# Upper parts first: token-major and expert products take the upper part of a weight load for all its chunks, then its lower part

## The chip, the core and the metric

One NeuronCore of one Trainium2 chip runs the whole kernel. The metric is the device time of one execution in microseconds (us), given as the median of three runs. TensorE is PE in all rows (PEld is its weight load), VectorE is DVE, ScalarE is ACT, GpSimd is POOL, SyncE (which issues the weight loads) is SP. L1717 is line 1717 of the kernel before.

## What is computed

Two transformer layers on 256 tokens of width 1024, in float32. Each layer has three token mixers (gated delta rule, dilated window attention, stick-breaking attention) between an input and an output projection, then a feed-forward part, which is dense in layer 0 and a mixture of 8 experts, two to a token, in layer 1, and then a gate:

```python
for i in range(DEPTH):
    hn = rms_norm(h, attn_norm_w[i])
    h = h + token_mixers(hn, w_in[i], ..., w_out[i])
    hn = rms_norm(h, ffn_norm_w[i])
    if i % 2 == 0:
        h = h + swiglu(hn, ffn_w1[j], ffn_w3[j], ffn_w2[j])
    else:
        h = h + moe_swiglu(hn, router_w[j], moe_w1[j], moe_w3[j], moe_w2[j])
    gate = jax.nn.sigmoid(rms_norm(h, ple_norm_w[i]) @ ple_gate[i])
    h = h + (p[i] @ ple_proj[i]) * gate
return rms_norm(h, final_norm_w)
```

## The kernel before, in words

**Weights in two parts.** Weights stream in loads of 1 MB (128 partitions x 2048 float32) through a ring of six slots, 421 loads in all, of which 336 belong to the experts. For each load ACT writes the upper part `whi` (the value rounded to fp32r, `split_upper`, L622, semaphore `s_hi`, "weights_upper_part_ready"), then DVE writes the rest `wlo = raw - whi` (`split_lower`, L626, semaphore `s_lo`, "weights_split"). The activations are split in the same way into `xh` and `xl`. A product of two such numbers is three matmuls, written out in `product` (L1717 to L1719): upper with upper, upper with lower, lower with upper, all added in one PSUM bank. With token-major operands the activation is the stationary one (loaded by PEld), and the weights move through, 512 (or 396, 384, 256) columns at a time. Rows name these three matmuls `whi,xh`, `wlo,xh` and `whi,xl`.

**The wait.** Before a load's first product PE waits once, in `ready` (L631), for `s_lo`, that is for the lower part, which comes after the upper part.

**Who takes which load.** `both_blocks` multiplies one 512-column group of weights with both blocks of 128 tokens; its eight chunks of the contraction come in two loads ("halves"), four chunks in each. It serves the token-major part of the input projection (J, three groups in a layer), the second half of the output projection (WO) and the gate (PG, two groups): 12 calls, 24 loads. In the experts an item is 128 gathered tokens of one expert. `up` (kinds A and B, seven 512-wide column groups j each) multiplies the gathered tokens with a half of four chunks, twice per group; `down` (kind C, seven groups) multiplies the gated product, turned to chunk-major by four transposes in `turn` (L2090), with a half that feeds both output banks YY0 and YY1. That is 42 loads and 504 matmuls in an item. There are 8 items: seven pass through a loop (`rest_of_item("each")`), the last stands behind it (`rest_of_item("last")`). The loop is turned so that A and B of group 0 of the next item run near the end of this one; A of group 0 stands right behind the last `turn`, ahead of the last `down`. The remaining users of loads (`channels`, the dense layer, the first half of WO, `ple`'s PP) are untouched by the change.

**Order around it.** ACT and DVE run one queue each, in which the splits stand between the drains of PSUM at places fixed by the plan (`Split.behind`). SP issues load n+6 when PE has finished with load n (a signal at the end of a half, or a filled PSUM tile).

Of the kernel before, what the change touches and what calls it, by code (L numbers as in the profile page):

```python
# [15 lines left out]
P = 128  # L16
# [379 lines left out]
def build(nc, x, stream, experts, columns, rows, final_w, consts, out):  # L396
# [9 lines left out]
    with ExitStack() as ctx:  # L406
# [222 lines left out]
        def ready(eng, key, it=None):  # L629

            eng.wait_ge(s_lo, through(load_at[key] + 1, it, per_load))  # L631

# [1054 lines left out]
        def _(pe):  # L1687
# [32 lines left out]

            def x_part(start, width):
                return xh[:, start:start + width], xl[:, start:start + width]

            def both_blocks(keys, name, width, items=None, turned=None):


                for half in range(2):
                    ready(pe, name + (half,), items)
                    for b, key in enumerate(keys):
                        if half == 0:  # L1730
                            opened(key, items)
                        for q in range(4):
                            k = 4 * half + q
                            if b == 0:
                                chunk_ready(turned, k, items)
                            ins = product(bank(key, 0, width), x_part(T * k + P * b, P),
                                          weights(name + (half,), width * q, width), k == 0, k == KC - 1)
                        if half:
                            ins.then_inc(s_fill, 1)
                    if half == 0:  # L1740
                        ins.then_inc(s_used, 1)
# [335 lines left out]
            def up(kind, ph, j, it):  # L2077
                key = (kind, ph, j)
                opened(key, it)
                for half in range(2):  # L2080
                    ready(pe, key + (half,), it)
                    for q in range(4):
                        k = 4 * half + q
                        ins = product(bank(key), x_part(P * k, P), weights(key + (half,), 512 * q, 512), k == 0, k == KC - 1)
# [8 lines left out]
            def down(ph, j, it):  # L2093
# [4 lines left out]
                for half in range(2):  # L2098
                    ready(pe, ("C", ph, j, half), it)
                    for m in range(2):  # L2100
                        for q in range(2):
                            c = 2 * half + q
                            ins = product(bank(("YY", ph, m)), (mTh[j % 2][:, P * c:P * c + P], mTl[j % 2][:, P * c:P * c + P]),
                                          weights(("C", ph, j, half), D * q + 512 * m, 512), j == 0 and c == 0,
                                          j == NJ - 1 and c == 3)
# [140 lines left out]
```

## Time and profile before

| | us |
|---|---|
| median of three runs | 1720.54 (1720.02 to 1720.63) |
| profiled execution, device time | 1722.51 |
| profiled execution, span of the trace | 1720.8 |
| PE busy, share of the span | 1635.3, 95% |
| PE weight load busy | 1392.9, 81% |
| DVE busy | 1296.5, 75% |
| ACT busy | 1047.9, 61% |
| POOL busy | 144.8, 8% |
| mean granted TensorE clock | 0.974 of full |

The profile is of one execution. Its span runs from the first to the last instruction; the device time is 1.7 us more than that. A matmul's busy time in a row is longer than its pace, since matmuls overlap: the pace is read from the start times of neighbouring rows. The stages by time: mixers of layer 0 to about 223 us, dense layer to about 421, gate and mixers of layer 1 to about 657, router and the first gather to about 681, experts to about 1669, gate and final norm to the end.

### The profile page before, as it was taken

The page shows a single profiled execution, that of the slowest core. Times are in us where ns is not written, and L with a number is a line of the kernel's source. Part 1 is how long each engine was busy: PE and PEld are TensorE (multiplying, and loading weights), DVE is VectorE, ACT ScalarE, POOL GpSimd, SP SyncE. Part 2 cuts the span into 40 slices and gives each one's busy share as a digit, 9 for nine tenths or more (in the row PEclk, how much of TensorE's full clock was granted, in tenths as well). Part 3 has the DMA queues.
Part 4 walks back from the last instruction along what each step waited for, and adds up shares of the span by engine and source line. Part 5 has one row for each costly group of instructions (what it writes and reads, how often), then busy time and mean ns, then how long its engine had stood idle before and what let it go on. Part 6 is the DMA issues. An engine that isn't in the chain of part 4 may idle for free.

```text
span 1720.8 us, 23469 instructions
## 1 busy us (share of the span) xinstructions
PE 1635.3 (95%) x8812; PEld 1392.9 (81%) x8812; DVE 1296.5 (75%) x1214; ACT 1047.9 (61%) x1005; POOL 144.8 (8%) x131
## 2 busy tenths in 40 slices
PE   6999989999899986999999999999999999999986
PEld 6989789998798975788887887887878878877864
DVE  4976555556687666788888888888888888888964
ACT  5646243334574724667676767677777767676743
POOL 0134100000012511000000000001000000002000
PEclk9999899999999998999999999999999999999998
DMA  7440154545444012999999999999999999999970
GB/s 287 169 149 1 50 202 178 199 169 220 151 168 171 2 49 86 370 365 357 389 363 360 382 367 359 380 358 382 367 358 383 367 348 392 367 351 411 368 275 25
DMA packets 65713, 459.91 MB, mean 267 GB/s; under 512 B 7408, under 2 KB 7792, under 8 KB 11632
## 3 DMA queue, kind: packets, MB, share of 16 engines
q1 hardware_dynamic: 61904, 445.88, 67.9%
q0 software_dynamic: 3744, 13.13, 2.0%
q8 instruction: 45, 0.74, 0.2%
q14 instruction: 20, 0.16, 0.0%
HBM read 450.58 MB, written 8.40 MB: 267 GB/s over the span
## 4 chain that ended last, share of the span: by engine, by line
PE 89%; DVE 4%; ACT 4%; POOL 1%; DMA 1%; issue 1%; DVEq 0%; POOLq 0%; ACTq 0%; SPq 0%
PE ps L1717 26%; PE ps L1719 26%; PE ps L1718 26%; PE ps L1835 2%; DVE wlo L626 2%; PE ps L1844 2%; ACT whi L622 1%; PE ps L2090 1%; PE ps L1904 1%; ACT xh L1036 1%; PE ps L1833 1%; DMA raw<-in_experts 1%; PE ps L1705 1%; POOL work L747 1%; PE ps L1816 0%
## 5 line engine op out<-in xcount | busy, mean ns | idle before, releaser
L626 DVE TENSOR_TENSOR wlo<-raw,whi 128x2048 fp32r<-128x2048 f32 x421 | 944.8, 2289 | 114.9 <-ACT whi L622 114.6
L622 ACT CAST whi<-raw 128x2048 fp32r<-128x2048 f32 x421 | 782.7, 1916 | 59.3 <-DMA raw<-in_experts 58.9
L1717 PE MATMUL ps<-whi,xh 128*128 128x512 f32 (+3 forms) x1568 | 623.1, 397 | 31.9 <-DVE wlo L626 20.0
L1718 PE MATMUL ps<-wlo,xh 128*128 128x512 f32 (+3 forms) x1568 | 616.3, 393 | 0.0
L1719 PE MATMUL ps<-whi,xl 128*128 128x512 f32 (+3 forms) x1568 | 616.0, 393 | 0.0
L1717 PEld LDWEIGHTS ps<-whi,xh 128*128 128x128 f32 x1568 | 297.6, 190 | 101.2 <-DVE wlo L626 17.3
L1719 PEld LDWEIGHTS ps<-whi,xl 128*128 128x128 f32 x1568 | 297.4, 190 | 67.1
L1718 PEld LDWEIGHTS ps<-wlo,xh 128*128 128x128 f32 x1568 | 298.0, 190 | 64.3
L1717 PE MATMUL ps<-xh,whi 128*128 128x256 f32 x656 | 186.2, 284 | 0.0
L1719 PE MATMUL ps<-xh,wlo 128*128 128x256 f32 x656 | 184.7, 282 | 0.0
L1718 PE MATMUL ps<-xl,whi 128*128 128x256 f32 x656 | 184.7, 282 | 0.0
L1047 ACT ACTIVATE work<-ps 128x512 f32<-128x512 f32 x56 | 33.5, 599 | 200.8 <-PE ps L1719 200.8
L1717 PEld LDWEIGHTS ps<-xh,whi 128*128 128x128 f32 x656 | 123.8, 189 | 1.3 <-issue 0.5
L1718 PEld LDWEIGHTS ps<-xl,whi 128*128 128x128 f32 x656 | 123.7, 189 | 1.4 <-issue 0.5
L1719 PEld LDWEIGHTS ps<-xh,wlo 128*128 128x128 f32 x656 | 123.6, 188 | 0.0
L1125 DVE TENSOR_TENSOR xl<-ps,xh 128x512 fp32r<-128x512 f32 x64 | 44.0, 690 | 73.5 <-ACT xh L1051 63.9
L1013 ACT ACTIVATE work<-ps 128x256 f32<-128x256 f32 x22 | 8.4, 384 | 111.5 <-PE ps L1719 111.5
L747 POOL TENSOR_TENSOR work<-work,cst 128x384 f32<-128x384 f32 x56 | 65.9, 1205 | 95.8 <-PE ps L1825 73.1
L788 POOL DMA_DIRECT2D y_rows<-work x7 | 4.0, 569 | 786.7 <-ACT work L1080 786.7
L1454 DVE TENSOR_TENSOR work<-work,ps 128x256 f32<-128x256 f32 x22 | 9.3, 421 | 67.2 <-ACT work L1013 67.2
L1835 PE MATMUL ps<-work 128*128 128x128 f32 x288 | 44.5, 300 | 1.3 <-POOL work L747 1.0
L957 ACT COPY work<-ps 128x384 f32<-128x384 f32 x48 | 23.1, 482 | 36.5 <-PE ps L1835 33.7
(275 smaller groups left out, 1304.8 us busy)
## 6 DMA issues: line engine op xcount, KB each, us to landing
raw<-in_experts SPq DMA_DIRECT2D x336, 1024.0 KB, 4.8
raw<-in_stream SPq DMA_DIRECT2D x85, 1024.0 KB, 4.9
y_rows<-work POOLq DMA_DIRECT2D x7, 512.0 KB, 5.2
y_rows<-work POOLq DMA_DIRECT2D x1, 2560.0 KB, 9.1
cst<-in_consts SPq DMA_DIRECT2D x1, 1383.5 KB, 13.6
h<-in_x SPq DMA_DIRECT2D x1, 1024.0 KB, 5.0
x_rows<-hn POOLq DMA_DIRECT2D x1, 1024.0 KB, 4.4
out<-work SPq DMA_DIRECT2D x2, 512.0 KB, 2.7
```

The source lines that it names most:

```text
L622: nc.scalar.copy(whi[:, n % RING, :], raw[:, n % RING, :]).then_inc(s_hi, 1)
L626: nc.vector.tensor_tensor(wlo[:, n % RING, :], raw[:, n % RING, :], whi[:, n % RING, :].bitcast(F32), ALU.subtract).then_inc(s_lo, 1)
L747: nc.gpsimd.tensor_tensor(cm[:, GW * g:GW * g + GW].rearrange("p (s i) -> p s i", s=3), mt[:, GW * g:GW * g + GW].rearrange("p (s i) -> p ...
L957: nc.scalar.copy(pbuf[:, at], bank(("P", L, lev, g), 0, GW)).then_inc(s_free["a"], 1)
L1036: ins = nc.scalar.activation(xh[:, P * k:P * k + P], bank(("GA", when, half), P * q, P), ACT.Copy, scale=col(COL_NORM(4) + k))
L1047: nc.scalar.activation(ms[j % 2], bank(key), ACT.Silu).then_inc(s_free["a"], 1)
L1125: nc.vector.tensor_tensor(lo, bank(key), hi.bitcast(F32), ALU.subtract).then_inc(s_free["v"], 1)
L1717: pe.matmul(out, ah, bh, start=start, stop=False)
L1718: pe.matmul(out, ah, bl, start=False, stop=False)
L1719: return pe.matmul(out, al, bh, start=False, stop=stop)
L1835: ins = pe.matmul(bank(key, P * s, P), lhs[:, at], rhs[:, at], start=True, stop=True)
L1844: ins = pe.matmul(packed(bank(key, P // 2 * s, P // 2), lev), lhs[:, at], joined(rhs[:, at], lev, odd), start=True, stop=True)
```

## The change

`product` is split in two for the token-major and the expert products. `upper_products` does the two matmuls of a chunk that read `whi`; `lower_product` does the one that reads `wlo`. For each half, PE waits for `s_hi` (new `upper_ready`), runs the upper products of all its chunks, waits for `s_lo`, and then runs the lower products. In `both_blocks` the lower wait stands behind the upper products of the first token block alone; in `up` behind four chunks (8 matmuls); in `down` behind both output banks (8 matmuls). The number of matmuls and weight loads is as before; only the order of the sums changes.

```diff
+        def upper_ready(eng, key, it=None):
+
+            eng.wait_ge(s_hi, through(load_at[key] + 1, it, per_load))
...
+            def upper_products(out, x, w, start):
+
+                (xu, xd), (wu, _) = x, w
+                pe.matmul(out, xu, wu, start=start, stop=False)
+                return pe.matmul(out, xd, wu, start=False, stop=False)
+
+            def lower_product(out, x, w, stop):
+                return pe.matmul(out, x[0], w[1], start=False, stop=stop)
...
                 for half in range(2):
-                    ready(pe, name + (half,), items)
+                    upper_ready(pe, name + (half,), items)
                     for b, key in enumerate(keys):
                         if half == 0:
                             opened(key, items)
@@
                             k = 4 * half + q
                             if b == 0:
                                 chunk_ready(turned, k, items)
-                            ins = product(bank(key, 0, width), x_part(T * k + P * b, P),
-                                          weights(name + (half,), width * q, width), k == 0, k == KC - 1)
+                            upper_products(bank(key, 0, width), x_part(T * k + P * b, P),
+                                           weights(name + (half,), width * q, width), k == 0)
+                        if b == 0:
+                            ready(pe, name + (half,), items)
+                        for q in range(4):
+                            k = 4 * half + q
+                            ins = lower_product(bank(key, 0, width), x_part(T * k + P * b, P),
+                                                weights(name + (half,), width * q, width), k == KC - 1)
                         if half:
                             ins.then_inc(s_fill, 1)
...
                 for half in range(2):
+                    upper_ready(pe, key + (half,), it)
+                    for q in range(4):
+                        k = 4 * half + q
+                        upper_products(bank(key), x_part(P * k, P), weights(key + (half,), 512 * q, 512), k == 0)
                     ready(pe, key + (half,), it)
                     for q in range(4):
                         k = 4 * half + q
-                        ins = product(bank(key), x_part(P * k, P), weights(key + (half,), 512 * q, 512), k == 0, k == KC - 1)
+                        ins = lower_product(bank(key), x_part(P * k, P), weights(key + (half,), 512 * q, 512), k == KC - 1)
                     ins.then_inc(s_fill if half else s_used, 1)
...
                 for half in range(2):
+                    upper_ready(pe, ("C", ph, j, half), it)
+
+                    def turned_part(q):
+                        c = 2 * half + q
+                        return mTh[j % 2][:, P * c:P * c + P], mTl[j % 2][:, P * c:P * c + P]
+
+                    for m in range(2):
+                        for q in range(2):
+                            upper_products(bank(("YY", ph, m)), turned_part(q), weights(("C", ph, j, half), D * q + 512 * m, 512),
+                                           j == 0 and half == 0 and q == 0)
                     ready(pe, ("C", ph, j, half), it)
                     for m in range(2):
                         for q in range(2):
-                            c = 2 * half + q
-                            ins = product(bank(("YY", ph, m)), (mTh[j % 2][:, P * c:P * c + P], mTl[j % 2][:, P * c:P * c + P]),
-                                          weights(("C", ph, j, half), D * q + 512 * m, 512), j == 0 and c == 0,
-                                          j == NJ - 1 and c == 3)
+                            ins = lower_product(bank(("YY", ph, m)), turned_part(q),
+                                                weights(("C", ph, j, half), D * q + 512 * m, 512),
+                                                j == NJ - 1 and half == 1 and q == 1)
```

The order of PE's instructions at the places that the prediction speaks of follows; `weights_upper_part_ready` is `s_hi`, `weights_split` is `s_lo`, REGISTER_ALU works out a wait's value inside the loop of items. PE, the second half of an expert group in the loop, before:

```order
L631 REGISTER_ALU
L1717 MATMUL ps<-whi,xh 128x512 [waits weights_split]
L1718 MATMUL ps<-wlo,xh 128x512
L1719 MATMUL ps<-whi,xl 128x512
L1717 MATMUL ps<-whi,xh 128x512
L1718 MATMUL ps<-wlo,xh 128x512
L1719 MATMUL ps<-whi,xl 128x512
```

The same place in the changed kernel:

```order
L635 REGISTER_ALU
L1728 MATMUL ps<-whi,xh 128x512 [waits weights_upper_part_ready]
L1729 MATMUL ps<-whi,xl 128x512
L1728 MATMUL ps<-whi,xh 128x512
L1729 MATMUL ps<-whi,xl 128x512
L1728 MATMUL ps<-whi,xh 128x512
L1729 MATMUL ps<-whi,xl 128x512
L1728 MATMUL ps<-whi,xh 128x512
L1729 MATMUL ps<-whi,xl 128x512
L1732 MATMUL ps<-wlo,xh 128x512 [waits weights_split]
L1732 MATMUL ps<-wlo,xh 128x512 x3
```

The wait for the lower part has moved behind eight matmuls, and no further REGISTER_ALU stands ahead of it. PE, the last `down` of the last item, its second half with the scatter matmul (L2140 before, L2172 after) behind it, in the changed kernel:

```order
L635 REGISTER_ALU
L1728 MATMUL ps<-whi,xh 128x512 [waits weights_upper_part_ready]
L1729 MATMUL ps<-whi,xl 128x512
...
L1732 MATMUL ps<-wlo,xh 128x512 [waits weights_split]
L1732 MATMUL ps<-wlo,xh 128x512 x3
L594 REGISTER_ALU
L594 REGISTER_ALU [waits psum_drained_by_scalar]
L2172 MATMUL ps<-work 128x512 [waits psum_drained_by_scalar]
```

The four L1732 are two for YY0 and two for YY1, where before six matmuls of YY0 were followed by six of YY1; the scatter matmul behind them waits for ACT to have drained YY0, as before. PE, the first half of the gate's first group at the end of the kernel, changed:

```order
L635 REGISTER_ALU
L1699 REGISTER_ALU [waits weights_upper_part_ready]
L1699 REGISTER_ALU [waits psum_drained_by_scalar]
L1728 MATMUL ps<-whi,xh 128x512 [waits psum_drained_by_vector]
L1729 MATMUL ps<-whi,xl 128x512
...
L1732 MATMUL ps<-wlo,xh 128x512 [waits weights_split]
L1732 MATMUL ps<-wlo,xh 128x512 x3
L1699 REGISTER_ALU
L1728 MATMUL ps<-whi,xh 128x512 [waits psum_drained_by_vector,psum_drained_by_scalar]
```

Here the first wait of the chain is for the upper part where it was for the lower one; the lower one stands ahead of the last four matmuls of token block 0.

## Rows read from the trace of the kernel before

**Rows 1.** Waits of PE: us in total, times, longest us

```profile
PE ps L1717 <- DVE wlo L626: 20.0, 12, 6.2
```

**Rows 2.** The same, 677 to 1660 us (the experts without their end)

```profile
PE ps L1717 <- DVE wlo L626: 4.0, 9, 0.7
```

**Rows 3.** Windows: stretch, us, busy (x) of PE, PEld, DVE, ACT, POOL, clock, DMA share, GB/s

```profile
922.10:1044.30 122.20, 121.77 (x541) 98.24 (x541) 104.58 (x65) 87.70 (x67) 2.84 (x3) 1.00 0.96 369
```

**Rows 4.** Timeline of PE, two halves of an item: start us, us, instruction

```profile
902.74 0.39 PE L1719 MATMUL ps<-whi,xl 128*128 128x512 f32 x1
902.97 0.40 PE L1717 MATMUL ps<-whi,xh 128*128 128x512 f32 x1
...
908.34 0.39 PE L1719 MATMUL ps<-whi,xl 128*128 128x512 f32 x1
```

**Rows 5.** Timeline at an item's end, with [idle before <-releaser]

```profile
797.56 4.49 DVE L626 TENSOR_TENSOR wlo<-raw,whi 128x2048 fp32r<-128x2048 f32 x2 [0.67 <-ACT whi L622]
...
798.85 0.60 PE L2090 MATMUL ps<-cst,work 128*128 128x128 f32 x4
...
799.91 0.50 PE L1717 MATMUL ps<-whi,xh 128*128 128x512 f32 x1 [0.46 <-DVE wlo L626]
```

**Rows 6.** Timeline of PE, transposes with a product behind that waits for nothing

```profile
909.00 1.04 PE L2067 MATMUL ps<-cst,hn 128*128 128x128 f32 x8
909.79 0.48 PE L1717 MATMUL ps<-whi,xh 128*128 128x512 f32 x1
```

**Rows 7.** Timeline, last item, a half with a late load

```profile
1568.58 2.29 DVE L626 TENSOR_TENSOR wlo<-raw,whi 128x2048 fp32r<-128x2048 f32 x1 [2.58 <-ACT whi L622]
...
1569.80 0.40 PE L1719 MATMUL ps<-whi,xl 128*128 128x512 f32 x1
...
1570.92 0.50 PE L1717 MATMUL ps<-whi,xh 128*128 128x512 f32 x1 [0.72 <-DVE wlo L626]
```

**Rows 8.** Timeline, first weights of the kernel

```profile
16.78 6.70 DVE L626 TENSOR_TENSOR wlo<-raw,whi 128x2048 fp32r<-128x2048 f32 x3 [0.91 <-ACT whi L622]
...
19.12 0.70 PE L1717 MATMUL ps<-whi,xh 128*128 128x396 f32 x1 [5.04 <-DVE wlo L626]
```

**Rows 9.** Windows, start of the kernel

```profile
18.01:24.84 6.83, 5.71 (x17) 5.72 (x18) 6.83 (x4) 4.21 (x3) 0.00 (x0) 0.50 0.92 385
```

**Rows 10.** Timeline, the last item's last down

```profile
1658.21 4.49 DVE L626 TENSOR_TENSOR wlo<-raw,whi 128x2048 fp32r<-128x2048 f32 x2 [1.11 <-ACT whi L622]
...
1660.56 0.80 PE L1717 MATMUL ps<-whi,xh 128*128 128x512 f32 x1 [4.80 <-DVE wlo L626]
...
1661.15 0.63 PE L1718 MATMUL ps<-wlo,xh 128*128 128x512 f32 x1
...
1661.57 0.63 PE L1719 MATMUL ps<-whi,xl 128*128 128x512 f32 x1
```

**Rows 11.** Timeline, end of that down: drain of YY0, scatter matmul

```profile
1667.79 0.59 ACT L1080 COPY work<-ps 128x512 f32<-128x512 f32 x1 [4.21 <-PE ps L1719]
...
1668.97 1.88 PE L2140 MATMUL ps<-work 128*128 128x512 f32 x4
```

**Rows 12.** Timeline, first weights of the last gate

```profile
1683.36 6.70 DVE L626 TENSOR_TENSOR wlo<-raw,whi 128x2048 fp32r<-128x2048 f32 x3 [0.75 <-ACT whi L622]
...
1685.98 0.76 PE L1717 MATMUL ps<-whi,xh 128*128 128x512 f32 x1 [6.20 <-DVE wlo L626]
```

**Rows 13.** Timeline of PE, dense layer, where each L1717 opens another bank

```profile
267.30 0.40 PE L1719 MATMUL ps<-whi,gl 128*128 128x512 f32 x1
267.53 0.40 PE L1717 MATMUL ps<-whi,gh 128*128 128x512 f32 x1
```

**Rows 14.** Windows around idle times of PE

```profile
192.10:198.92 6.82, 5.96 (x16) 4.77 (x17) 2.75 (x5) 0.00 (x0) 4.24 (x3) 0.50 0.00 0
622.58:629.40 6.82, 4.50 (x30) 3.84 (x30) 5.59 (x10) 1.07 (x2) 4.15 (x4) 1.00 0.00 0
...
1659.82:1663.23 3.41, 2.67 (x6) 2.17 (x7) 3.41 (x3) 3.41 (x3) 0.00 (x0) 0.50 0.00 0
```

## Prediction

> **What bounds the kernel.** I read the waits of PE first, since PE is busy for 95% of the span. All the idle time that the change can touch is the time in which PE waited for the lower part of a load: 20.0 us in 12 waits [rows 1]. Next I asked where those 12 are. Nine lie inside the experts and make only 4.0 us [rows 2]; the other three are 5.0, 4.8 and 6.2 us long, one at the kernel's start, one at the last item's last `down`, one at the last gate; their rows stand with their terms. So the experts, which take more than half of the time, are bound by PE's own work: in an item of 122.20 us PE is busy for 121.77 at full clock, while DVE has 104.58, ACT 87.70, and the DMA engines are close to busy at 0.96 [rows 3]. The pace of that work is in start times: 24 products in a row take 5.60 us, 0.233 us each [rows 4]. Nothing in the change removes a matmul, so the gain is in waits and in what the waits do to the clock.
>
> **What the change does to a wait.** ACT has the upper part ready when DVE starts on the lower one, and DVE needs 2.3 us for it. So PE may start up to 2.3 us earlier, if nothing else holds it, and then has eight matmuls (1.9 us at full clock) to run before it needs the lower part. Where DVE had long finished, nothing is gained.
>
> **Term 1, the items, 4.9 us.** Behind the last four transposes of an item stands group A 0 of the next. Its lower part is made from 797.56 on, two loads in 4.49 us, so the first is ready at about 799.85, and PE starts at 799.91 [rows 5]. Its upper part was there at 797.5. The row shows 0.46 us of idle time, but the stall is longer: where nothing is waited for, a product starts 0.79 us after the first of eight transposes [rows 6], so after the first of four it is about 0.36, and 798.85 + 0.36 = 799.21. The stall is 0.70 us. The difference, 0.24, is the time in which a product normally overlaps the matmul ahead. There are seven such places (the other two of the nine are term 2): 7 x 0.70 = 4.9 us. It stays gained if the item has no other wait 0.7 us behind this one. The next half's lower part is there at 802.05 [rows 5], and PE, which comes to that half 12 x 0.233 = 2.8 us after its start, at 802.0, then needs it only 1.9 us later: the cover grows in every half. DVE and ACT have 17 and 34 us to spare in an item.
>
> **Term 2, a late load in the last item, 1.4 us.** The load's lower part starts at 1568.58 and PE, whose last product started at 1569.80, goes on at 1570.92 instead of 1570.03 [rows 7]: 0.89 us. The ninth wait is 4.0 - 7 x 0.43 - 0.72 = about 0.25 in the waits' account, with the 0.24 of term 1 about 0.5. Both upper parts are early enough. Together 1.4.
>
> **Term 3, the kernel's start, 2.3 us.** The upper part is ready at 16.78; PE would start there and not at 19.12 [rows 8]. Against this stand two things. The lower wait is reached after eight matmuls and the lower part comes at about 19.07, so PE stalls again for about 0.5 us. And the clock: from 18.01 to 24.84 the granted clock is 0.50, that is 1.2 GHz, 17 matmuls in 5.71 us or 0.336 each [rows 9]; at full clock I estimate 0.186. With the same low stretch after the change: 8 matmuls by 18.54, then 17.5 in 19.07 to 24.84, 25.5 against 17, 8.5 x 0.186 = 1.6 us. If the clock is back halfway, since PE is now busy through the whole stretch: 3.1 us. If it never falls: 4.1. I take 2.3, between the first two.
>
> **Term 4, the last down, 2.3 us.** Upper part at 1658.21, PE started at 1660.56 [rows 10]: 2.3 us earlier again, at two paces: 0.42 us a matmul at 1.2 GHz [rows 10] against 0.233. Same low stretch (1659.82 to 1666.65): 6.4 matmuls before it, 16 in it, and its 24 end at about 1667.0 instead of 1668.97 [rows 11]: 1.9 us. Clock back at 1663.2: 3.5. No fall: 4.7, of which I count 4.2, since in the code DVE has two more loads to split ahead of the residual sums. From each goes 0.4 us: YY0 used to be full six matmuls ahead of the end, so that ACT's drain of 0.59 us was hidden [rows 11]; now it is two matmuls ahead, and the scatter matmul waits. So 1.5, 3.1 or 3.8; I take 2.3.
>
> **Term 5, the last gate, 2.2 us.** Upper part at 1683.36, PE started at 1685.98, 0.3 us after the lower part was ready, through a chain of waits that stays [rows 12]. New start 1683.7. Same low stretch (1683.72 to 1690.54): 5.3 more matmuls in it and the first one earlier, 1.6 us. Clock back halfway: 2.8. No fall: 4.4. I take 2.2.
>
> **What costs nothing.** The 360 loads concerned (336 + 24) get one more wait on PE each, and the order of the changed kernel shows no extra register instruction ahead of it. A wait that is met costs nothing now: between the last product of a half and the first of the next, which carries a wait, lie 0.23 us like anywhere [rows 4]. New is that two matmuls in a row read the same weights. No row has that; the nearest are the two paces of 512 columns, 0.233 [rows 4] and 0.23 in the dense layer [rows 13], which differ by about 1 ns. On 4032 + 576 = 4608 matmuls 1 ns is 4.6 us, up or down. I take 0 and keep part of it for the range.
>
> **A rule that speaks against it.** In `down` the bank changes three times in a half instead of once. In the dense layer every third matmul opens another bank, and the step to it is 0.23 us, at full clock [rows 13]. The Trainium skill (TensorE: Matmul & The Clock Gate, "A second HAM failure mode: psum-queue depth-cycling") says that cycling through PSUM banks made PE pause between groups so often that its clock went down and up. By that rule some of the halves of `down` would run at 0.42 us a matmul instead of 0.233. This trace doesn't agree: the rule's term is 0 here.
>
> **Sum.** 4.9 + 1.4 + 2.3 + 2.3 + 2.2 = 13.1 us. The profiled execution took 1722.51 us, so it would take 1709.4; the median of the runs shown, 1720.54, lies 1.97 lower, so the forecast is 1707.4. With all low stretches as they are: 1.6 + 1.5 + 1.6 + 6.3 = 11.0 us, 1709.5.
>
> **Rivals.**
> *The clock never falls at the three places.* PE's idle time there goes from 5.0, 4.8 and 6.2 us to 2.7, 2.5 and 3.9. What 2.3 us does is undecided: of two idle times of 2.32 us behind the same code, one is followed by 1.2 GHz (192.10 to 198.92) and the other isn't (622.58 to 629.40) [rows 14]. Against it: at 1659.82 the clock stayed low although PE was busy for 2.67 of 3.41 us [rows 14]. Gain 4.1 + 3.8 + 4.4 + 6.3 = 18.6, 1701.9 us. Chance 0.2, for two of three or all.
> *The items keep their period.* DMA at 0.96 and the order of ACT and DVE could pace the item, so that the 0.70 us comes back as a wait for an upper part. For it: the DMA share [rows 3]. Against it: PE's work alone explains the item, and the wait at its end is all there is. Gain 13.1 - 4.9 = 8.2, 1712.3 us. Chance 0.1.
> *The second wait breaks PE's pipeline: slower.* If the weight load that carries the lower wait could no longer overlap the matmul ahead, each of 360 loads would cost the 0.10 us by which a matmul behind a real wait is longer (0.50 against 0.40) [rows 4, 5]: 36 us, less 13, 1743 us. It decides from 0.05 us a load on. Against it: the met wait at 902.97 [rows 4]. A slower pace of the new order, from 4 ns a matmul on, would end on the same side. Chance 0.07.
> *Gain and a small loss of pace cancel*, 2.5 ns a matmul: within 0.2%, 1720 us, chance 0.05.
>
> **Numbers.** A measurement of this kernel can tell about 0.2%, 3.4 us. The forecast has 0.58, the rivals 0.2, 0.1, 0.07, 0.05. Elsewhere the low stretches may fall otherwise once all work comes 2 us earlier; one more or less of 6.8 us is 3.0 us. The range goes from the first rival, 1701.5, to the smallest gain, 1709.5, with one more low stretch and some loss of pace, 1714.0. Faster 0.88, same 0.05, slower 0.07.
>
> **What would show it.** Right: an item of 121.5 us and no wait of PE for a lower part in it; the first J product at 16.8, with a wait for L626 of about 0.5 us behind eight matmuls; the last gate's first product 2.3 us behind ACT's split start and not 4.6; ACT's drain of YY0 visible ahead of the scatter matmul. Wrong: an item of 122.2 with waits for `whi`, or a step between start times other than 0.233, which moves everything.

## The result, and the profile after

| | before | changed |
|---|---|---|
| median of the runs made together on one chip | 1720.59 us (4 runs) | 1711.2 us (4 runs, 1708.2 to 1713.3) |
| the same, second comparison on another chip | 1719.0 us (17 runs) | 1710.41 us (6 runs, 1707.1 to 1713.2) |
| profiled execution, device time | 1722.51 | 1710.77 |
| its span | 1720.8 | 1709.0 |

PE's line of the profile's page, which answers to 1635.3 and 95% before:

```profile
PE 1632.8 (96%) x8812; PEld 1391.7 (81%) x8812; DVE 1296.2 (76%) x1214; ACT 1048.8 (61%) x1005; POOL 152.7 (9%) x131
```

The ratio is 0.9944 (95% interval 0.9930 to 0.9957), and 0.9948 (0.9935 to 0.9961) the second time: faster by 9.4 and by 8.6 us, where 13.1 were forecast. The time lies in the range, 3.8 us above the forecast.

Waits of PE in the changed kernel (us in total, times, longest us), which answer to [rows 1]; L1728 is the upper product, L1732 the lower one:

```profile
PE ps L1728 <- ACT whi L622: 9.1, 3, 3.9
...
PE ps L2172 <- ACT work L1084: 0.2, 1, 0.2
PE ps L1732 <- DVE wlo L626: 0.2, 1, 0.2
```

20.0 us in 12 waits for a lower part have become 9.1 us in three waits for an upper part, and 0.2 for a lower one. The three are the three long ones of before; the nine of [rows 2] are gone but for that 0.2. Here they are in the timeline (start us, us, instruction, idle before and its releaser), first the kernel's start, which answers to [rows 8]:

```profile
16.68 6.70 DVE L626 TENSOR_TENSOR wlo<-raw,whi 128x2048 fp32r<-128x2048 f32 x3 [0.91 <-ACT whi L622]
...
16.70 0.45 PE L1728 MATMUL ps<-whi,xh 128*128 128x396 f32 x1 [2.72 <-ACT whi L622]
...
18.07 0.53 PE L1729 MATMUL ps<-whi,xl 128*128 128x396 f32 x1
...
18.40 0.53 PE L1728 MATMUL ps<-whi,xh 128*128 128x396 f32 x1
...
19.06 1.65 PE L1732 MATMUL ps<-wlo,xh 128*128 128x396 f32 x4
```

PE starts 0.02 us after the upper part is complete (the moment at which DVE starts on the lower part), and reaches the first lower product at 19.06 without a wait. Windows (stretch, us, busy (x) of PE, PEld, DVE, ACT, POOL, granted clock, DMA share, GB/s) of this place, of the last `down`, of the last gate and of one item; they answer to [rows 9], [rows 14] and [rows 3]:

```profile
17.30:20.70 3.40, 3.40 (x12) 3.10 (x11) 3.40 (x2) 3.40 (x3) 0.00 (x0) 0.50 1.02 429
20.70:24.10 3.40, 3.40 (x21) 3.40 (x20) 3.40 (x3) 1.44 (x1) 0.00 (x0) 1.00 1.01 422
908.48:1029.99 121.51, 121.51 (x543) 98.22 (x542) 104.66 (x64) 87.85 (x67) 4.99 (x3) 1.00 0.97 371
1652.20:1655.60 3.40, 3.05 (x7) 2.49 (x8) 3.07 (x2) 3.40 (x3) 0.00 (x0) 0.51 0.82 328
1676.10:1679.50 3.40, 3.40 (x10) 2.60 (x9) 3.40 (x3) 3.40 (x3) 0.00 (x0) 0.51 0.02 5
```

In this execution the clock falls to 1.2 GHz for 3.4 us and not for 6.8 at all three places: the middle case of each of terms 3 to 5. Other executions differ, as the part on the prediction shows. The item takes 121.51 us, and PE is busy in all of it. The end of an item, which answers to [rows 5]:

```profile
797.72 4.50 DVE L626 TENSOR_TENSOR wlo<-raw,whi 128x2048 fp32r<-128x2048 f32 x2 [0.66 <-ACT whi L622]
...
799.04 0.60 PE L2113 MATMUL ps<-cst,work 128*128 128x128 f32 x4
...
799.40 0.48 PE L1728 MATMUL ps<-whi,xh 128*128 128x512 f32 x1
```

The product starts 0.36 us after the first of the four transposes, with no idle time, and now ahead of the lower part, which is complete at about 799.97. The late load of the last item [rows 7], the last `down` and its scatter matmul [rows 10, 11], and the last gate [rows 12]:

```profile
1573.89 1.19 PE L1732 MATMUL ps<-wlo,xh 128*128 128x512 f32 x4 [0.20 <-DVE wlo L626]
```

```profile
1652.53 8.90 DVE L626 TENSOR_TENSOR wlo<-raw,whi 128x2048 fp32r<-128x2048 f32 x4 [1.10 <-ACT whi L622]
...
1652.55 0.80 PE L1728 MATMUL ps<-whi,xh 128*128 128x512 f32 x1 [2.47 <-ACT whi L622]
...
1659.37 1.07 ACT L1084 COPY work<-ps 128x512 f32<-128x512 f32 x2 [1.45 <-PE ps L1732]
...
1660.01 2.41 PE L2172 MATMUL ps<-work 128*128 128x512 f32 x5 [0.21 <-ACT work L1084]
```

```profile
1672.55 3.75 ACT L622 CAST whi<-raw 128x2048 fp32r<-128x2048 f32 x2
1674.52 2.29 DVE L626 TENSOR_TENSOR wlo<-raw,whi 128x2048 fp32r<-128x2048 f32 x1 [0.75 <-ACT whi L622]
...
1674.82 0.47 PE L1728 MATMUL ps<-whi,xh 128*128 128x512 f32 x1 [3.87 <-ACT whi L622]
```

What remains of the long waits is the part that ends with ACT. In the last rows ACT starts on the load at 1672.55 only. That it isn't the load that is late but ACT's other work of this place was tried (gate_ahead, below).

### The profile page after: what moved, and what is told of

Same layout as the page of the kernel before. It is cut to its first block, busy times and chain, and to the rows that moved or that the text cites. A ratio compares the mean times of both kernels' runs of the same rounds, so it can differ in the third digit from the quotient of the medians.

```text
span 1709.0 us, 23469 instructions
## 1 busy us (share of the span) xinstructions
PE 1632.8 (96%) x8812; PEld 1391.7 (81%) x8812; DVE 1296.2 (76%) x1214; ACT 1048.8 (61%) x1005; POOL 152.7 (9%) x131
## 4 chain that ended last, share of the span: by engine, by line
PE 93%; ACT 2%; DVE 2%; DMA 1%; issue 1%; POOL 1%; DVEq 0%; POOLq 0%; ACTq 0%; SPq 0%
PE ps L1728 21%; PE ps L1732 20%; PE ps L1729 20%; PE ps L1721 6%; PE ps L1723 6%; PE ps L1722 6%; PE ps L1854 2%; PE ps L1863 2%; PE ps L2113 1%; PE ps L1923 1%; PE ps L1852 1%; DMA raw<-in_experts 1%; ACT whi L622 1%; ACT xh L859 1%; PE ps L1709 1%
## 5 line engine op out<-in xcount | busy, mean ns | idle before, releaser
L1728 PE MATMUL ps<-whi,xh 128*128 128x512 f32 (+2 forms) x1536 | 610.2, 398 | 14.3 <-ACT whi L622 9.1
L1729 PE MATMUL ps<-whi,xl 128*128 128x512 f32 (+2 forms) x1536 | 597.1, 389 | 0.0
L1732 PE MATMUL ps<-wlo,xh 128*128 128x512 f32 (+2 forms) x1536 | 415.2, 392 | 0.2 <-DVE wlo L626 0.2
L1728 PEld LDWEIGHTS ps<-whi,xh 128*128 128x128 f32 x1536 | 290.4, 189 | 83.2 <-issue 7.5
L1732 PEld LDWEIGHTS ps<-wlo,xh 128*128 128x128 f32 x1536 | 287.1, 189 | 66.6 <-DVE wlo L626 1.1
L1729 PEld LDWEIGHTS ps<-whi,xl 128*128 128x128 f32 x1536 | 290.6, 189 | 59.0
```

The source lines that it names most:

```text
L1728: pe.matmul(out, xu, wu, start=start, stop=False)
L1729: return pe.matmul(out, xd, wu, start=False, stop=False)
L1732: return pe.matmul(out, x[0], w[1], start=False, stop=stop)
```

## The experiments

Twelve further runs were made: of nine new kernels, and once more of the changed kernel and of two of the nine. Each was timed against the kernel before on the same chip, so that differences are to be read against the "before" of the same line. One execution of each run has a trace. The table has the pieces of time between marks that all traces have: the start of the last token-major matmul of layer 0's input projection ("J"), the transposes of the tokens of the second item ("G") and of the eighth, which are the bounds of six items, the last `turn`, the scatter matmul behind the last `down`, the transposes of the last gate's norm, and the end. "Low" is the time at 1.2 GHz between 24 and 690 us, good to 0.3 us, without what is left of the start's own low stretch. Each other number is a difference of two start times, in us.

| kernel | 0 to J | J to G | low | six items | to last turn | to scatter | norm to end |
|---|---|---|---|---|---|---|---|
| before | 105.14 | 681.7 | 61.2 | 733.18 | 135.16 | 13.81 | 42.89 |
| order_only | 104.34 | 681.2 | 61.2 | 731.38 | 134.63 | 13.42 | 42.15 |
| order_again | 103.78 | 680.4 | 61.2 | 732.82 | 134.93 | 12.76 | 43.42 |
| x_start | 103.47 | 681.9 | 61.2 | 731.70 | 135.12 | 12.65 | 42.32 |
| x_down | 104.81 | 681.6 | 57.8 | 731.75 | 135.36 | 9.60 | 42.08 |
| x_up | 104.25 | 681.2 | 61.2 | 728.40 | 134.14 | 13.08 | 42.38 |
| x_rest | 104.21 | 681.0 | 64.7 | 729.00 | 132.88 | 10.68 | 40.91 |
| changed | 101.84 | 685.1 | 68.0 | 729.04 | 133.47 | 10.53 | 39.98 |
| after_again | 102.14 | 683.6 | 68.1 | 729.00 | 132.88 | 9.60 | 40.04 |
| gate_ahead | 102.70 | 685.3 | 68.0 | 729.04 | 132.88 | 10.69 | 35.17 |
| both_ahead | 103.01 | 682.3 | 61.2 | 729.04 | 133.42 | 8.12 | 35.17 |
| warm | 102.71 | 680.6 | 44.2 | 729.00 | 132.88 | 9.60 | 40.05 |
| best | 101.73 | 681.2 | 51.0 | 729.04 | 132.88 | 8.13 | 35.16 |
| best_again | 101.74 | 680.5 | 51.0 | 729.00 | 132.88 | 8.12 | 35.17 |

### The change, one part at a time

Each of these four kernels has the changed form for some callers, and for the others the loops of the kernel before, with `ready` ahead of everything and `product`. The condition is written into `both_blocks`, the expert product and `down`; here it is for x_start:

```diff
             def both_blocks(keys, name, width, items=None, turned=None):
+                if not (name == ("J", 0, 0)):
+                    for half in range(2):
+                        ready(pe, name + (half,), items)
...
+                                ins = product(bank(key, 0, width), x_part(T * k + P * b, P),
+                                              weights(name + (half,), width * q, width), k == 0, k == KC - 1)
...
+                    return
```

**x_start**: only the kernel's first input projection group is changed.

> The change in the first J product of layer 0 alone; everything else waits as before. Theory (each wait gives back what it cost, and low-clock stretches between 113 and 695 us then fall as chance has it): the first product starts at 16.7 instead of 19.1, 1.6 to 3.2 us gained by the first POOL wait at 110 to 112, one low-clock stretch more or less after that, time 1717 to 1721, and PE waits for L626 in the experts as before (item 122.20). Rival (the new order itself costs pace): 1720.5, no gain at 112 either.

Measured: 1717.07 us against 1720.71 of before, ratio 0.9976 (0.9967 to 0.9984), 3.6 us faster, at the lower end of the expected 1717 to 1721. PE starts at 16.93, and J comes 1.7 us earlier than in the trace of the kernel before, but only 1.0 us earlier than on the mean of the six traces with the late start (104.4). Where the rest of the 3.6 us comes from, the one trace doesn't show.

**x_up**: only the expert products (kinds A and B).

> The change in the expert products A and B alone. Theory: the seven waits at the items' starts and the two in the last item go, item 121.51 instead of 122.20, gain 4.8 + 1.4 = 6.2 us, about 1714.4; first 695 us of the trace as before; the last down and the last gate still start behind the lower part. Rival (pace): the item is longer than 121.51, since its 336 matmuls of A and B run in the new order.

Measured: 1714.25 us, ratio 0.9967 (0.9952 to 0.9982), 6.5 us faster. An item of it, in the columns of the windows above:

```profile
785.47:907.00 121.53, 121.53 (x543) 98.24 (x542) 104.47 (x64) 87.71 (x67) 4.92 (x3) 1.00 0.96 372
```

The six items take 728.4 us; the item is short with `up` alone, as the theory of the seven stalls says, since the group behind an item's last `turn` is one of `up`. The time is the one expected (1714.4), but of the two waits in the last item only one went: at 1573.33 us PE still waits 1.10 us for the lower part of a `down` half.

**x_down**: only `down`.

> The change in the expert products C alone. Theory: item 122.20 as before, only the last down gains, 1.5 to 3.3 us, 1717.3 to 1719; ACT's drain of YY0 shows ahead of the scatter matmul. Rival (bank changes cost): the item is longer than 122.20 by some ns for each of 14 x 2 further bank changes, 0.3 us or more.

Measured: 1717.19 us, ratio 0.9979 (0.9969 to 0.9988), 3.5 us faster, 0.1 us more than the expectation allowed. From the last turn to the scatter matmul it takes 9.60 us; the three kernels that leave this `down` as it was take 12.65 to 13.81. The items take 731.75, in the middle of the four kernels of which PE waits at each item's end (731.38 to 733.18), so `down` gives an item nothing. The 122.20 of the expectation is then too exact a number: an item that nothing has changed, in x_start, has 121.84 to 122.11.

**x_rest**: all but the kernel's first group.

> The whole change without the first J product of layer 0. Theory: the first 680 us as in the kernel before (same waits, same low-clock stretches), then 6.2 + 3.3 + 2.8 = 12.3 us less, about 1708.3, with a smaller spread between runs than the whole change has; then the start's 3.2 us were lost again by the clock in between. Rival (the middle is slower through the new order in J, WO and PG): 1711 or more, and the middle loses time with the start unchanged.

Measured: 1713.54 us, ratio 0.9959 (0.9945 to 0.9973), 7.2 us faster and not 12. The items, the last `down` and the gate have what they have in the changed kernel, 922.5 us from G to the end against 922.05 there. But the expectation was that without the earlier start the clock's pattern would stay that of before, and that the runs would agree better. They don't: five runs lie between 1709.4 and 1715.4. The time is the rival's (1711 or more), while its sign, a slower middle, does not show in the trace: J to G takes 681.0 us. But the traced execution is the fastest of the five, 11.3 us below the kernel before, and the longer ones left no trace. So some 5 us of what the parts promise are missing here too, without the earlier start.

### The order without the earlier start

```diff
         def upper_ready(eng, key, it=None):
 
-            eng.wait_ge(s_hi, through(load_at[key] + 1, it, per_load))
+            eng.wait_ge(s_lo, through(load_at[key] + 1, it, per_load))
```

PE then waits for the lower part ahead of the upper products, so that the order of the products is all that is left of the change. **order_only**:

> The changed kernel's order of products, but PE waits for the lower part ahead of the upper products, as the kernel before did. Theory: the whole gain is the earlier start, and the order (two matmuls in a row on the same weights, four banks changed in a down half instead of two) costs and brings nothing: pace 0.233 us in the items, item period 122.2, the three long waits 5.0, 4.8 and 6.2 us again, time that of the kernel before within 2 us plus up to 1 us for the scatter matmul, which now waits for ScalarE's drain. Rival: the order itself has a price or a gain per matmul, 4608 of them: 0.5 ns is 2.3 us, an item period off by 0.25 us.

Measured: 1724.41 us (12 runs, 1717.85 to 1726.37) against 1719.0, ratio 1.0026 (1.0017 to 1.0035): slower by 5.4 us, which the theory didn't have. But the profiled one was the fastest of the twelve, and shows nothing slow: the three long waits are back, and the items take 731.38. So it was run again, as **order_again**:

> The order without the earlier start once more, since its one profiled execution (1717.85 us) was the fastest of its 12 and the others (1720.1 to 1726.4) had a mean granted clock down to 0.970. Theory: the slower executions lose in low stretches between 24 and 690 us and at the three long waits, not in the experts: item period again 121.9 to 122.2, low time above the 61.2 us of the profiled one by 3 to 14 us, the first 690 us longer by 1 to 5 us than there. Rival: the order makes the experts slower in those executions: item period above 122.4.

Measured: 1720.3 us (12 runs, 1716.3 to 1726.8) against 1719.45, ratio 1.0009 (0.9994 to 1.0023): no difference that can be measured. The profiled execution (1718.87 us) is again not one of the longer ones, which it was meant to catch. What the two traces tell is the pace. The waits of PE in order_only:

```profile
PE ps L1728 <- DVE wlo L626: 19.8, 11, 6.2
```

Two items next to each other in order_only, then one of order_again, then one of the kernel before:

```profile
907.38:1029.20 121.82, 121.38 (x542) 98.59 (x541) 104.44 (x64) 87.73 (x67) 3.16 (x3) 1.00 0.96 370
1029.20:1151.38 122.18, 121.73 (x542) 98.28 (x541) 104.53 (x64) 87.61 (x67) 3.33 (x3) 1.00 0.96 369
```

```profile
906.00:1028.18 122.18, 121.72 (x542) 98.27 (x541) 104.58 (x64) 87.81 (x67) 3.32 (x3) 1.00 0.95 369
```

```profile
786.82:909.00 122.18, 121.72 (x542) 98.27 (x541) 104.56 (x64) 87.73 (x67) 3.19 (x3) 1.00 0.96 369
```

An item of the kernel before and one with the new order alone take the same 122.18 us, with 121.72 of work on PE in both. So the order, the two matmuls in a row on the same weights and the additional changes of the bank cost nothing in the experts, and bring nothing: the 0.5 to 0.7 us of an item are the earlier start. This holds for the experts. Open is why 8 of the 12 executions of order_only and 4 of the 12 of order_again are at 1723.5 to 1726.8 us. Their mean granted clock is 0.970 to 0.975 and that of the others, at 1716.3 to 1721.2, is 0.976 to 0.982, so the time goes with the clock; but none of these 12 left a trace. That the new order brings such executions about more often, outside the experts, is a rival that no run here excludes.

### Where the 3 to 4 us went

**after_again**: the changed kernel again.

> The changed kernel once more, on the chip of the other two. Theory: its low stretches between 24 and 690 us do not come to the same sum each time, so that its runs spread over some 5 us (1708 to 1713 so far), 8 to 11 us below the kernel before. Rival: they are fixed by the program, and the profile shows 68 us of low time with the same 11 stretches again and the segments agree to 0.3 us.

Measured: 1710.41 us, ratio 0.9948 (0.9935 to 0.9961). Here the rival was mostly right: low time comes to 68.1 us again, and 0 to J, J to G and the items agree with the first trace to 0.3, 1.5 and 0.04 us. The seven traces of kernels that lack part of the change take 680.4 to 681.9 us from J to G; the four traces whose code up to G is the changed kernel's take 685.1, 683.6, 685.3 and 682.3, on the mean 2.8 us more. The one with 682.3 (both_ahead) is also the one whose low time is 61.2 and not 68. In their one trace each, neither the earlier start alone (x_start, 681.9) nor the rest alone (x_rest, 681.0) does this.

The traces also show where most of it goes. In the output projection of each layer, four transposes are followed by 2.32 us of idle time and twelve matmuls, up to the next transposes. In layer 1 the changed kernel takes 8.19 us for this:

```profile
619.44 0.61 PE L1968 MATMUL ps<-cst,hn 128*128 128x128 f32 x4
622.37 0.77 PE L1721 MATMUL ps<-whi,xh 128*128 128x512 f32 x1 [2.33 <-issue]
...
627.63 1.34 PE L1968 MATMUL ps<-cst,hn 128*128 128x128 f32 x8
```

and the kernel before 6.12, with the matmuls at full clock [rows 14]:

```profile
624.04 0.61 PE L1949 MATMUL ps<-cst,hn 128*128 128x128 f32 x4
626.97 0.48 PE L1717 MATMUL ps<-whi,xh 128*128 128x512 f32 x1 [2.32 <-issue]
...
630.16 1.06 PE L1949 MATMUL ps<-cst,hn 128*128 128x128 f32 x8 [0.15 <-DVE hn L1378]
```

The same stretch in all 14 traces, in us:

| traces | layer 0 | layer 1 | J to G |
|---|---|---|---|
| before, x_start, x_down, both_ahead | 8.2 | 6.1 | 681.6 to 682.3 |
| order_only, order_again, x_up, x_rest, best, best_again | 6.1 | 8.2 | 680.4 to 681.2 |
| changed, after_again, gate_ahead | 8.2 | 8.2 | 683.6 to 685.3 |
| warm | 8.2 | 7.1 | 680.6 |

The ten traces of the first two lines have 1.2 GHz at one of the two places, the three with 68 us of low time at both. That is 2.1 us of the 3.4 by which these three exceed the seven. both_ahead has the same code up to there and the low clock at one place only, so the program does not fix it.

**warm**: products that nobody reads, issued where PE waits for a norm, to see what the low stretches behind these waits cost.

```diff
                     if c == 0:
+                        for _ in range({1: 4, 3: 5, 4: 4}.get(occ, 0)):
+                            pe.matmul(bank(("T", occ, 0)), ident, cst[:, 0:512], start=True, stop=True)
                         pe.wait_ge(s_hn["a"], occ + 1)
```

> The changed kernel with 4, 5 and 4 extra products of 128 x 512 on TensorE into an unused bank, issued where PE waits for the norms ahead of the second, fourth and fifth sets of norm transposes (the profile shows a granted clock of 0.50 for 3.4 to 6.8 us behind each of these waits). Their results are read by nothing. Theory that the idle wait ahead is what the lower clock follows, and that a low stretch costs 0.45 us for each of its us: the stretches behind these three waits go or halve, low time between 24 and 690 us falls from 68 to 50 to 57 us, and the time falls by 3 to 8 us, to 1703 to 1708. Rival: the low stretches come from something else or only move to another place: low time stays within 5 us of 68, time at 1711 or up to 3 us above it for the extra work where it outlasts the wait.

Measured: 1706.54 us against 1718.84, ratio 0.9927 (0.9911 to 0.9944), 12.3 us faster than before, which is 3.3 us more than the changed kernel's gain (9.0, the mean of 9.4 and 8.6). Low time falls to 44.2 us, and J to G to 680.6. So the stretches behind these waits do follow PE's idle time. But 24 us less of low time bring only 4.1 us (684.7 to 680.6 from J to G, the first being the mean of the three traces with 68 us), 0.17 us for each, where the expectation had 0.45. One of the three places shows why; the changed kernel first, then warm, PE alone:

```profile
448.02 3.26 PE L1709 MATMUL ps<-cst,hn 128*128 128x128 f32 x16 [5.60 <-ACT hn L853]
```

```profile
448.02:452.54 4.52, 4.52 (x24) 4.42 (x25) 2.52 (x7) 3.36 (x9) 0.00 (x0) 0.70 0.01 2
```

```profile
448.48 1.97 PE L1711 MATMUL ps<-cst,hn 128*128 128x128 f32 x16 [1.26 <-ACT hn L853]
451.18 0.42 PE L1730 MATMUL ps<-whi,xh 128*128 128x396 f32 x1 [0.73 <-DVE xl L1121]
```

```profile
448.48:453.00 4.52, 3.79 (x26) 3.58 (x27) 2.96 (x8) 3.83 (x9) 0.00 (x0) 1.00 0.01 2
```

At 1.2 GHz the 16 transposes take 3.26 us and the product behind them waits for nothing. At full clock they take 1.97, and the product waits 0.73 us for DVE's lower part of the activations. Behind a norm DVE and ACT bound the stretch, and PE's clock is mostly not what it costs. In a stream of products it is: a product starts 0.42 us after the last instead of 0.233 [rows 10, 4]. Part of warm's 4.1 us lies away from the added products: 1.0 us of it is layer 1's stretch of the table above.

### What could be had on top

In the changed kernel the two long waits at the end are for ACT, and by the order of ACT's queue for nothing else: its splits stand behind other work. `ahead` lets `Split` do loads before their usual place.

```diff
+            def ahead(self, count, it=None):
+
+                for _ in range(count):
+                    self.one(self.next, it)
+                    self.next += 1
...
                 if ph == "each":
                     split.behind(("YY", ph, 1), it)
                     split.behind(("B", ph, 0), it)
+                else:
+                    split.ahead(1, it)
...
                             add_to_residual(("SC", b, m), b, m, it)
+                    split.ahead(1, it)
```

**gate_ahead** is this edit on the changed kernel.

> The changed kernel, but ScalarE and VectorE split the first load of the last gate before the copies of the last down product and the residual sums that stood ahead of them. Theory: in the changed kernel PE idles 3.87 us on ScalarE's upper part ahead of the last gate only because these 15 or so operations stand in front of it; with them behind, the gate's first product starts as soon as the last load's input is there, its idle falls to 0.7 us or less, and the time from the start of the last set of norm transposes to the end falls by 3.2 us, or by up to 5 if the clock does not fall there either: 1706 to 1708 against the changed kernel's 1711.2. Rival: the input of the last load itself, the normalised activations, is what comes late, so the wait stays near 3 us and the time within 1 us of 1711.2. Second rival: the copies moved behind are awaited by the output, so that what the gate gains the tail behind it gives back: idle gone, end within 1 us.

Measured: 1704.5 us against 1718.84, ratio 0.9907 (0.9888 to 0.9926). From the last norm to the end 35.17 us, where the changed kernel took 40.0: 4.8 less, near the upper end of the expectation. The gate's first product in it:

```profile
1672.15 0.47 PE L1737 MATMUL ps<-whi,xh 128*128 128x512 f32 x1 [0.62 <-DVE xl L1129]
```

The idle time fell from 3.87 to 0.62 us and is now for the activations; the clock stays at 2.4 GHz behind it.

**both_ahead** has the splits ahead of the last `turned` as well:

```diff
                 else:
                     scatter_matrix(it)
+                    split.ahead(2, it)
                 turned(ph, NJ - 1, it)
...
                     split.behind(("B", ph, NJ - 1), it, most=2)
+                else:
+                    split.ahead(2, it)
                 turned(ph, NJ - 1, it)
```

> As the run before, and the last down product's first two loads are split ahead of the last output normalisation on both engines. Theory: the 2.47 us that PE idles on the upper part ahead of the last down product goes, for 2 to 3.5 us more: 1703 to 1705.5. Rival: the loads' own input (the last gated products) is made by the same engines just before, so that nothing can be taken ahead and what is moved only delays the normalisation: PE's wait moves behind the last transposes, time as gate_ahead's within 1 us or up to 2 us longer.

Measured: 1700.85 us, ratio 0.9893 (0.9872 to 0.9913), 3.7 us below gate_ahead. The first product of the last `down`:

```profile
1649.83 0.49 PE L1740 MATMUL ps<-whi,xh 128*128 128x512 f32 x1 [1.48 <-DVE xl L1138]
```

1.48 us of idle time instead of 2.47, now for DVE's lower part of the turned product, at full clock again: from the last turn to the scatter matmul 8.12 us instead of 9.6 (the traces in which the clock does not fall there either) to 10.7.

**best** is both_ahead and warm together.

> All three edits on top of the changed kernel. If they are independent the gains add: gate's 3.2 to 5, the last down's 2 to 3.5 and the clock's 3 to 8, so 1695 to 1703. If the low stretches only move about when one is taken away, the sum comes out above that by what the clock gives back, 1703 to 1707.

Measured: 1698.82 us (4 runs, 1698.1 to 1699.1) against 1718.84, ratio 0.9878 (0.9856 to 0.9899). On another chip, as **best_again**:

> The three edits together once more, beside the changed kernel on one chip: 1697 to 1700 if its four earlier runs (1698.1 to 1699.1) stand, that is 11 to 13 us below the changed kernel; 1701 to 1706 if those fell in a favourable pattern of low stretches.

Measured: 1698.76 us against 1719.0, ratio 0.9883 (0.9868 to 0.9897), where the changed kernel beside it had 1710.41. It is 11.7 us faster than the changed kernel and 20.2 faster than before. The gains nearly add: 9.0 (the change), 5.3 (gate), 3.7 (last `down`) and 3.3 (warm) make 21.3, against 20.0 and 20.2. And the runs agree to 2 us, where those of the kernel before spread over 5 to 8.

## Why the prediction was right, and where it was off

Against the forecast of 13.1 us stand the pieces of the table. For each I compare means, since one trace of each kernel was not enough: that of the kernel before is the slowest of its like in three of the six columns.

- **What bounds the kernel, and what a wait costs.** Right. The experts are bound by PE's work, the gain is in the waits, and the second wait is free: x_up's item has 121.53 us of work in 121.53 us. The rival in which the items keep their period and the one in which the second wait breaks PE's pipeline are excluded by the same row.
- **Term 1, 4.9 us, and term 2, 1.4 us.** Right, slightly too high. Six items take 729.0 us instead of 732.3 on the mean of before, x_start and the two order runs: 0.54 us an item and not 0.70. The 0.70 was right for the trace it was read from (122.20 against 121.51); items with the wait come in two lengths, below. The seventh stall and the late load, 0.7 + 1.4 = 2.1, brought 134.96 - 133.02 = 1.9 (the means of those four and of the eight traces in which the experts are changed as a whole), in two of the eight with a wait of 0.20 for the lower part left.
- **Term 3, the start, 2.3 us.** Right: 0 to J is 102.3 us on the mean of the seven traces with the whole change at the start, 104.4 on that of the six with the late start, 2.2 us less (2.15). The wait of 0.5 us behind eight matmuls came in one of the seven traces, warm, in which the clock fell with the last of the eight:

```profile
19.23 1.69 PE L1734 MATMUL ps<-wlo,xh 128*128 128x396 f32 x4 [0.48 <-DVE wlo L626]
```

  In the changed kernel's trace it did not come, as the clock fell within the eight, at 17.30 and not at 18.01, and PE took until 19.06 for them.
- **Term 4, the last down, 2.3 us.** It brought 3.1: 13.2 on the mean of before, x_start and x_up, and 10.1 on that of the six traces with the changed `down` and the old place of the split. It was mis-sized in the clock alone, and the 3.1 is a mean of two cases: in three of the six traces (changed, x_rest, gate_ahead; 10.53 to 10.69) the clock is back after 3.4 us, for which 3.1 was worked out, and in the other three (x_down, after_again, warm; 9.60 each) it doesn't fall there at all, for which the first rival had 3.8. The scatter matmul waits for ACT's drain as foreseen, for 0.21 us.
- **Term 5, the last gate, 2.2 us.** Right: 42.5 on the mean of the six without it, 40.2 of the four with it: 2.3.
- **Pace 0.** Right, by order_again's item. The rule of the Trainium skill (TensorE: Matmul & The Clock Gate, "A second HAM failure mode: psum-queue depth-cycling") on cycling through PSUM banks stays without effect here: no low stretch starts between 690 and 1640 us in any trace.
- **What failed: the middle, which was left at 0.** The prediction noted that low stretches "may fall otherwise once all work comes 2 us earlier" and kept that for the range, at 3.0 us for one more stretch of 6.8 us. In the changed kernel low time from 24 to 690 us is 68 us in three of four traces instead of 61.2, and J to G takes 2.8 us more on the mean of the four. It gives back more than the start brought. The largest piece of it stood in the prediction's own rows: behind the same 2.32 us of idle time the clock fell in layer 0 and not in layer 1 [rows 14], and in the three traces it falls in both, for 2.1 us. Everything together: 2.2 + 3.3 + 1.9 + 3.1 + 2.3 - 2.8 = 10.0 us, against 9.4 and 8.6 measured.

Each of the forecast's terms was found at its place, so that the gain is no luck; the time is above the forecast for the most part by what the middle gave back. What brings the extra low time about stays open. It is not the sum of low time as such that costs: x_rest has 64.7 us of it and warm 44.2, with 681.0 and 680.6 from J to G. Nor is the earlier start shown to be the cause: medians of x_start, x_up and x_down add up to 13.6 us without the gate's 2.3, and x_rest, which lacks the earlier start, still reaches 7.2 only. Its longer executions, like those of order_only, left no trace, so the new order stays a rival.

## What to carry to other kernels

Where an operand is made in two steps, let the consumer start with all that needs the first, and put the wait for the second behind it: the wait itself is free, and each stall behind it shrinks by up to the time of the work put ahead. Then look at what the stall is for now: here it was an engine's queue order, and two splits moved ahead brought as much again as the change. A gain of 2 us in the first 20 can be outweighed by one or two low-clock stretches more 170 to 600 us later, whatever their cause, so price each place by its own piece of the timeline and take such pieces from more than one trace.

## What the runs showed of the hardware

- **An item's pace has two values at the same granted clock.** In one execution of order_only an item takes 121.82 us and the next 122.18, with 121.38 and 121.73 of work on PE and clock 1.00 for both (rows above); the kernel before has 122.18 and five times 122.20, x_start, with the same experts, 121.84 to 122.11, and x_up 121.28 and 121.52 in turn. With the changed experts as a whole it is 121.47 to 121.51 in all eight traces. What sets it stays open.
- **The same idle time can be followed by either clock.** Behind the same code and 2.32 to 2.33 us of idle time of PE, in the output projections of the two layers, 17 of 28 stretches ran at 1.2 GHz (8.2 us), one partly (7.1) and 10 at 2.4 (6.1).
- **The price of low time differs a lot between places.** 0.17 us for each us of low time in warm, on the mean of all the places where it went; 0.30 in the output projections (2.07 us for 6.8); 0.45 in a row of products (1 - 0.233/0.42 = 0.45).
- **The start's low stretch lies differently in each execution.** In the changed kernel the first products start 0.29 and 0.18 us apart and only from 17.41 on 0.33, until 20.7; in both_ahead they are 0.33 apart until 22.8; in gate_ahead, with the same code there and the same 2.7 us of waiting ahead, they are 0.33 apart from the second to 21.46. Its trace has no record of the granted clock for this time, and the pace alone tells the clock. The products of 396 columns in gate_ahead:

```profile
17.50 0.53 PE L1737 MATMUL ps<-whi,xh 128*128 128x396 f32 x1
...
17.83 0.53 PE L1738 MATMUL ps<-whi,xl 128*128 128x396 f32 x1
...
21.46 0.43 PE L1737 MATMUL ps<-whi,xh 128*128 128x396 f32 x1
...
21.74 0.34 PE L1738 MATMUL ps<-whi,xl 128*128 128x396 f32 x1
```
